# Second unit's low half of each later gate and up half on GpSimd, and five seven-product units in every one of them

## The chip, the cores and the metric

One Trainium2 chip, one of its NeuronCores. The metric is the device time of one execution of the whole program in microseconds (us). Lower is better.

## The reference, cut to what matters

One layer of a residual block on 256 tokens: a half-step feed-forward network, a mixer (a gated recurrence and a short convolution between two projections) and a second half-step feed-forward network. The change touches the gate and up products of the two feed-forward networks only.

```python
D_MODEL = 2048; SEQ = 256; D_FF = 5632; DEPTH = 1
def swiglu(x, w_gate, w_up, w_down):
    return (jax.nn.silu(x @ w_gate) * (x @ w_up)) @ w_down
...
f = swiglu(rmsnorm(h, ffn1_pre_g[l]), ffn1_w_gate[l], ffn1_w_up[l], ffn1_w_down[l])
h = h + 0.5 * rmsnorm(f, ffn1_post_g[l])
...
f = swiglu(rmsnorm(h, ffn2_pre_g[l]), ffn2_w_gate[l], ffn2_w_up[l], ffn2_w_down[l])
h = h + 0.5 * rmsnorm(f, ffn2_post_g[l])
```

## The kernel before, in words

**Number format.** Every float32 operand of a product is split in a high part (a rounded copy, made by ScalarE) and a low part (the difference, made by VectorE). A product is then three matmuls on TensorE: high by high, high by low, low by high (`three`, line 1770). Each of them is a 128x128 block of activations against 512 columns of weights.

**Halves and units.** The first 512 columns of gate and up are made in a plain way. The other 5120 are made in five pairs of 1024 gate columns and 1024 up columns. Each pair has two halves, c = 0 to 9: even c is the gate half, odd c the up half. A half is eight units, p = 0 to 7. A unit is 256 rows of the weights by 1024 columns, taken as a 2x2 matrix of blocks B11, B12, B21, B22 (512 columns each, 1 MB in all), against the 2x2 matrix of the activations (two tiles of rows, two tiles of 128 tokens).

**Seven products or eight.** A plain unit is eight block products, so 24 matmuls. A unit listed in `SEVEN` (line 97) is made with a Strassen-like scheme of seven products, so 21 matmuls. Before the change a half has the seven-product units 2, 4, 6 (c = 0), 0, 2, 3, 4, 6 (c odd) or 0, 2, 4, 6 (c even and above 0). What a seven-product unit asks for beside the matmuls:

- the DMA queue loads B12 early, and then GpSimd issues a second DMA that adds B22's neighbour block into it from DRAM (`pair_sum`, line 689);
- VectorE makes three sums in `tsum` (`half_sums`, line 1235: one instruction of 128x512 and one of 128x1024);
- ScalarE rounds them into `t_hi` (`sums_hi`), VectorE makes `t_lo` (`sums_lo`, line 1250, 128x1536).

`tsum`, `t_hi` and `t_lo` have two places each. So the sums of a unit may be made only when TensorE has finished the seven-product unit two back in the list. That is the wait on `two_back(f, q, p)` (line 437) in `half_sums`.

**Every unit.** ScalarE makes `u_hi` (`half_hi`), VectorE `u_lo` (`half_lo`, line 1228, 128x2048, two inputs in SBUF). The raw weights have four places: the load of unit p waits until TensorE has finished unit p-4.

**VectorE's order in a half** (`half_steps`, line 1286), as written out by hand. First the seven additions of `bank_sums` (line 1255) for the half before, each of which reads one operand from PSUM and one from SBUF. They wait for TensorE at the end of the half before. Then `half_lo` of unit 1, the sums, low half and `t_lo` of unit 2, and so on to unit 7, and last the same for unit 0 of the next half. In gate halves with c above 0 there are two more instructions, `pair_hidden` (line 1193): the elementwise product of gate and up of the pair before. They stand in the order just ahead of `half_lo` of unit 2 and just ahead of `half_lo` of unit 4. TensorE transposes their result after units 3, 4, 5 and 6 of the same half (`pair_transpose`, four small matmuls each).

**GpSimd's order** in this phase is only the row of `pair_sum` DMAs, unit after unit (`pair_sums`, line 696).

**TensorE's order** (`half_unit`, line 1776): unit after unit. Each waits for its low half; the sixth product of a seven-product unit waits for `t_lo`.

The whole is run twice (f = 0 and 1), which makes 160 units and 88 seven-product units.

Of the kernel before, what the change touches and what calls it, by code (L numbers as in the profile page):

```python
# [23 lines left out]
def hybrid_block_kernel(nc, x, f1_pre, f1_wg, f1_wu, f1_wd, f1_post, mix_pre, w_in, conv_w, conv_b,  # L24
                        w_r, b_r, w_i, b_i, lam, sc_w, w_out, mix_post, f2_pre, f2_wg, f2_wu, f2_wd,
                        f2_post, out):
    f32, f32r = mybir.dt.float32, mybir.dt.float32r
    ALU, ACT, AX = mybir.AluOpType, mybir.ActivationFunctionType, mybir.AxisListType
# [13 lines left out]
    GP, GF = KD // GK, KF // GK  # L42
# [51 lines left out]
    HALVES = 2 * PAIRS  # L94
    UNITS = HALVES * GP
    TURN = 4
    SEVEN = [(2, 4, 6)] + [(0, 2, 3, 4, 6) if c % 2 else (0, 2, 4, 6) for c in range(1, HALVES)]
    LAST_SEVEN = SEVEN[0][-1]
    first_seven = [sum(len(x) for x in SEVEN[:c]) for c in range(HALVES + 1)]
    NS = first_seven[HALVES]  # L100
# [20 lines left out]
    EVAC = 7  # L121
# [17 lines left out]
    def lin(q, a, b):  # L139

        it, c = q
        return a * c + b if isinstance(it, int) else it * (TURN * a) + (a * c + b)
# [10 lines left out]
    with ctx:  # L153
# [3 lines left out]
        def sem(name):  # L157
            return ctx.enter_context(nc.semaphore(name))
# [58 lines left out]
        u_raw = [over(f"u_raw{n}", [P, 2, 4, W], f32, a) for n, a in enumerate((resid_at, ring_at))]  # L217
        u_lo = [over(f"u_lo{n}", [P, 2, 4, W], f32r, a) for n, a in enumerate((resid_at, ring_at))]
        u_hi = [over(f"u_hi{n}", [P, 2, 4, W], f32r, a) for n, a in enumerate((ring_at + 2 * ring, ring_at + ring))]
# [34 lines left out]
        def unit(ring_of, p):  # L254
            return ring_of[p % 4 // 2][:, p % 2]
# [89 lines left out]
        pair_raw = {p: sem(f"pair_raw{p}") for p in SEVEN[1]}  # L345
        unit_sum = {p: sem(f"unit_sum{p}") for p in SEVEN[1]}
        pair_used = sem("pair_used")
        unit_hi, unit_lo = sem("unit_hi"), sem("unit_lo")
        unit_used = sem("unit_used")
        sums_done = sem("sums_done")  # L350
        t_hi_done, t_lo_done = sem("t_hi_done"), sem("t_lo_done")
# [2 lines left out]
        evac = sem("evac")  # L354
# [49 lines left out]

        def unit_count(f, q, p):
            return lin(q, GP, UNITS * f + p + 1)

        def turns(q, a, b):

            it, c = q  # L410
            return b if isinstance(it, int) else it * a + b
# [211 lines left out]
        def _(pool):  # L623
# [65 lines left out]
            def pair_sum(f, q, p):  # L689

                first = W + 2 * W * (q // 2)
                pool.wait_ge(pair_raw[p], pair_count(f, (0, q), p))
                pool.dma_start(unit(u_raw, p)[:, B12], ffn_w[f][q % 2][:, GK * p + 1, first:first + W],
                               accum_op=ALU.add).then_inc(unit_sum[p], 16)

            def pair_sums(f):

                for q in range(HALVES):
                    for p in SEVEN[q]:
                        if (q, p) != (0, 2):  # L700
                            pair_sum(f, q, p)

            def down_pairs(f):

# [398 lines left out]
        def _(dve):  # L1103
# [124 lines left out]
            def half_lo(f, q, p):  # L1228
                dve.wait_ge(unit_hi, unit_count(f, q, p))
                if seven(q, p):  # L1230
                    dve.wait_ge(sums_done, sums_count(f, q, p))
                ve.tensor_tensor(unit(u_lo, p), unit(u_raw, p), unit(u_hi, p).bitcast(f32), ALU.subtract  # L1232
                                 ).then_inc(unit_lo, 1)
# [52 lines left out]
            def half_steps(f, q):  # L1286
                it, c = q
                prev, after = (it, c - 1), (it, c + 1)
                if c:
                    bank_sums(f, prev, range(EVAC))  # L1290
                else:
                    hidden(f)
                half_lo(f, q, 1)
                half_sums(f, q, 2)
                if c and c % 2 == 0:
                    pair_hidden(f, prev, 0)
                half_lo(f, q, 2)
                sums_lo(f, q, 2)
                if seven(q, 3):
                    half_sums(f, q, 3)  # L1300
                half_lo(f, q, 3)
                if seven(q, 3):
                    sums_lo(f, q, 3)
                half_sums(f, q, 4)
                if c and c % 2 == 0:
                    pair_hidden(f, prev, 1)
                half_lo(f, q, 4)
                sums_lo(f, q, 4)
                half_lo(f, q, 5)
                if c == 0:  # L1310
                    form_lo_of(f, 7, 8, 9)
                half_sums(f, q, 6)
                half_lo(f, q, 6)
                sums_lo(f, q, 6)
                half_lo(f, q, 7)
                if c < HALVES - 1:
                    seven_first(f, after)
# [336 lines left out]
        def _(pe):  # L1654
# [121 lines left out]
            def half_unit(f, q, p):  # L1776

                c = q[1]
                a12, a22, a11, a21 = ((xT_hi[:, 2 * p + k, part(t)], xT_lo[:, 2 * p + k, part(t)])
                                      for k in range(2) for t in range(2))  # L1780

                def form(name):
                    n = FORM[p, name]
                    return xf[:, n, 0], xf[:, n, 1]

                def raw_of(b):
                    return unit(u_hi, p)[:, b], unit(u_lo, p)[:, b]

                def plain(m, x1, b1, x2, b2):
                    three(bank(m), x1, *raw_of(b1), c == 0 and p == 0, False)  # L1790
                    return three(bank(m), x2, *raw_of(b2), False, p == GP - 1)

                pe.wait_ge(unit_lo, unit_count(f, q, p))
                if c == 0 and p < 3:
                    pe.wait_ge(form_lo, NF * f + (2, 4, 7)[p])
                elif c == 1 and p == 3:
                    pe.wait_ge(form_lo, NF * (f + 1))
                if not seven(q, p):
                    end = p == GP - 1
                    last = plain(M3, form("D1"), B12, form("D2"), B22)  # L1800
                    if end:
                        last.then_inc(bank_done, 1)
                    last = plain(M2, a11, B11, a12, B21)
                    if end:
                        last.then_inc(bank_done, 1)
                    last = plain(M5, a21, B12, a22, B22)
                    if end:
                        last.then_inc(bank_done, 1)
                    last = plain(M4, a21, B11, a22, B21)
                    last.then_inc(unit_used, 1)  # L1810
                    return
                first, end = p == SEVEN[c][0], p == SEVEN[c][-1]
                emptied = first and c > 0
                done = EVAC * (HALVES * f - 1)
                u = seven_sem(q, p)

                def sum_of(b):
                    return t_hi[u][:, b], t_lo[:, u, b]

                def m1():  # L1820
                    if emptied:
                        pe.wait_ge(m1_out, lin(q, 1, HALVES * f))
                    last = three(bank(M1), a11, *raw_of(B11), first, end)
                    if end:
                        last.then_inc(bank_done, 1)

                def m5():
                    if emptied:
                        pe.wait_ge(evac, lin(q, EVAC, done + 6))
                    three(bank(M5), form("S1"), *raw_of(B12), emptied, False).then_inc(pair_used, 1)  # L1830

                if not emptied:
                    m5()
                if not first or c:
                    m1()
                if emptied:
                    pe.wait_ge(evac, lin(q, EVAC, done + 3))
                three(bank(M2), a12, *raw_of(B21), emptied, False)
                if emptied:
                    pe.wait_ge(evac, lin(q, EVAC, done + 4))  # L1840
                three(bank(M3), form("S4"), *raw_of(B22), emptied, False)
                if emptied:
                    m5()
                if first and c == 0:
                    pe.wait_ge(silu_done, TOK * (f + 1))
                    m1()
                pe.wait_ge(t_lo_done, seven_count(f, q, p))
                last = three(bank(M6), form("S2"), *sum_of(U2), first, end)
                if end:
                    last.then_inc(bank_done, 1)  # L1850
                if emptied:
                    pe.wait_ge(evac, lin(q, EVAC, done + 7))
                three(bank(M4), a22, *sum_of(V4), emptied, False)
                if first and c == 0:
                    pe.wait_ge(hid_done, TOK * (f + 1))
                last = three(bank(M7), form("D1"), *sum_of(V3), first, end)
                last.then_inc(unit_used, 1)
# [202 lines left out]
```

## Time and profile before

| what | value |
|---|---|
| median of 3 runs | 1739.95 us (1738.59 to 1741.5) |
| the profiled execution | 1739.42 us |
| its span in the profile | 1737.6 us |
| TensorE matmuls, weight loads | 7728 each |
| share of the span busy: TensorE, VectorE, ScalarE, GpSimd | 99%, 85%, 57%, 10% |
| granted TensorE clock | 0.999 of full speed |

The profiled execution lasts 1.8 us longer than its span; what lies around the span is start and end. A matmul's record is 0.39 us long, but the next one starts 0.23 us after it: the records overlap, so TensorE's time is to be counted by starts, not by durations. VectorE's records overlap too, by about 0.1 us. A "gap" in TensorE is where the distance from one start to the next is more than 0.23 us.

### The profile page before, as it was taken

The page shows a single profiled execution, that of the slowest core. Times are in us where ns is not written, and L with a number is a line of the kernel's source. Part 1 is how long each engine was busy: PE and PEld are TensorE (multiplying, and loading weights), DVE is VectorE, ACT ScalarE, POOL GpSimd, SP SyncE. Part 2 cuts the span into 40 slices and gives each one's busy share as a digit, 9 for nine tenths or more (in the row PEclk, how much of TensorE's full clock was granted, in tenths as well). Part 3 has the DMA queues.
Part 4 walks back from the last instruction along what each step waited for, and adds up shares of the span by engine and source line. Part 5 has one row for each costly group of instructions (what it writes and reads, how often), then busy time and mean ns, then how long its engine had stood idle before and what let it go on. Part 6 is the DMA issues. An engine that isn't in the chain of part 4 may idle for free.

```text
span 1737.6 us, 21090 instructions
## 1 busy us (share of the span) xinstructions
PE 1721.0 (99%) x7728; PEld 1419.3 (82%) x7728; DVE 1470.5 (85%) x1297; ACT 993.3 (57%) x951; POOL 170.0 (10%) x160
## 2 busy tenths in 40 slices
PE   9999999999999999999999999999999999999997
PEld 7778888888888888788888888888888888888886
DVE  6999999999899877755685558999999999988786
ACT  7665656555656444756654447565656565655543
POOL 5300000000000000100000018001010111000000
PEclk9999999999999999999999999999999999999999
DMA  7788778787767667575565557787878787677665
GB/s 240 224 235 229 226 229 241 221 242 220 219 206 232 215 201 252 177 232 174 164 195 180 192 183 248 212 239 226 238 223 242 229 236 227 197 222 234 204 199 201
DMA packets 148517, 378.15 MB, mean 218 GB/s; under 512 B 12364, under 2 KB 14548, under 8 KB 147668
## 3 DMA queue, kind: packets, MB, share of 16 engines
q1 hardware_dynamic: 133716, 350.33, 61.6%
q0 software_dynamic: 14688, 26.75, 9.9%
q8 instruction: 49, 0.80, 0.2%
q14 instruction: 32, 0.26, 0.1%
q10 hardware_dynamic: 32, 0.01, 0.0%
HBM read 372.84 MB, written 4.19 MB: 217 GB/s over the span
## 4 chain that ended last, share of the span: by engine, by line
PE 93%; DVE 2%; DMA 2%; issue 1%; ACT 0%; POOL 0%; SPq 0%; DVEq 0%; ACTq 0%
PE ps L1772 23%; PE ps L1774 23%; PE ps L1773 23%; PE ps L1662 7%; PE ps L1664 7%; PE ps L1663 7%; PE ps L1767 1%; DMA u_raw<-in_ffn_w_gate 1%; DVE w_lo L1117 1%; DVE u_lo L1232 1%; DMA u_raw<-in_ffn_w_up 1%; PE ps L1981 1%; DMA raw<-in_ffn_w_gate 0%; PE ps L1993 0%; PE ps L1703 0%
## 5 line engine op out<-in xcount | busy, mean ns | idle before, releaser
L842 ACT CAST u_hi<-u_raw 128x2048 fp32r<-128x2048 f32 x160 | 305.8, 1913 | 167.0 <-DMA u_raw<-in_ffn_w_gate 80.7
L1232 DVE TENSOR_TENSOR u_lo<-u_raw,u_hi 128x2048 fp32r<-128x2048 f32 x160 | 367.4, 2296 | 11.6 <-ACT u_hi L842 4.5
L1117 DVE TENSOR_TENSOR w_lo<-raw,w_hi 128x1024 fp32r<-128x1024 f32 x156 | 195.9, 1262 | 134.4 <-ACT w_hi L743 132.3
L743 ACT CAST w_hi<-raw 128x1024 fp32r<-128x1024 f32 x160 | 166.7, 1052 | 138.1 <-PE ps L1664 111.5
L1772 PE MATMUL ps<-u_hi,xT_hi 128*128 128x512 f32 x608 | 237.0, 390 | 0.0
L1774 PE MATMUL ps<-u_hi,xT_lo 128*128 128x512 f32 x608 | 236.9, 390 | 0.0
L1773 PE MATMUL ps<-u_lo,xT_hi 128*128 128x512 f32 x608 | 236.7, 389 | 0.0
L1006 ACT CAST d_hi<-d_raw 128x2048 fp32r<-128x2048 f32 x80 | 152.8, 1913 | 115.9 <-DVE d_raw L1450 60.8
L1443 DVE TENSOR_TENSOR d_lo<-d_raw,d_hi 128x2048 fp32r<-128x2048 f32 x80 | 182.9, 2288 | 15.1 <-ACT d_hi L1006 12.0
L849 ACT CAST t_hi<-tsum 128x1536 fp32r<-128x1536 f32 x88 | 130.7, 1485 | 107.0 <-DVE tsum L1247 106.2
L1662 PE MATMUL ps<-w_hi,xT_hi 128*128 128x512 f32 x448 | 178.3, 398 | 2.6 <-DVE xT_lo L1153 2.3
L1772 PE MATMUL ps<-d_hi,hT_all 128*128 128x512 f32 x460 | 179.2, 390 | 0.0
L1774 PE MATMUL ps<-d_hi,hT_all 128*128 128x512 f32 x460 | 179.1, 389 | 0.0
L1773 PE MATMUL ps<-d_lo,hT_all 128*128 128x512 f32 x460 | 179.0, 389 | 0.0
L1664 PE MATMUL ps<-w_hi,xT_lo 128*128 128x512 f32 x448 | 174.9, 390 | 0.0
L1663 PE MATMUL ps<-w_lo,xT_hi 128*128 128x512 f32 x448 | 174.5, 390 | 0.0
L1253 DVE TENSOR_TENSOR t_lo<-tsum,t_hi 128x1536 fp32r<-128x1536 f32 x88 | 154.2, 1752 | 20.2 <-ACT t_hi L849 20.2
L1773 PEld LDWEIGHTS ps<-u_lo,xT_hi 128*128 128x128 f32 x608 | 114.2, 188 | 24.2
L1774 PEld LDWEIGHTS ps<-u_hi,xT_lo 128*128 128x128 f32 x608 | 114.2, 188 | 24.0
L1772 PEld LDWEIGHTS ps<-u_hi,xT_hi 128*128 128x128 f32 x608 | 114.2, 188 | 24.0
L1772 PE MATMUL ps<-u_hi,xf 128*128 128x512 f32 x320 | 129.1, 404 | 2.3 <-DVE u_lo L1232 1.2
L1774 PE MATMUL ps<-u_hi,xf 128*128 128x512 f32 x320 | 125.0, 391 | 0.0
(207 smaller groups left out, 3049.8 us busy)
## 6 DMA issues: line engine op xcount, KB each, us to landing
d_raw<-in_ffn_w_down SPq DMA_DIRECT2D x50, 1024.0 KB, 5.3
u_raw<-in_ffn_w_gate SPq DMA_DIRECT2D x42, 1024.0 KB, 5.2
raw<-in_w_in SPq DMA_DIRECT2D x80, 512.0 KB, 3.7
u_raw<-in_ffn_w_up SPq DMA_DIRECT2D x30, 1024.0 KB, 5.2
u_raw<-in_ffn_w_up SPq DMA_DIRECT2D x100, 256.0 KB, 4.2
u_raw<-in_ffn_w_up SPq DMA_DIRECT2D x50, 512.0 KB, 3.7
u_raw<-in_ffn_w_gate SPq DMA_DIRECT2D x76, 256.0 KB, 4.1
u_raw<-in_ffn_w_gate SPq DMA_DIRECT2D x38, 512.0 KB, 3.7
```

Of the source, the lines that this page charges most:

```text
L743: sc.copy(w_hi[:, s], raw[:, s]).then_inc(hi_ready, 1)
L842: sc.copy(unit(u_hi, p), unit(u_raw, p)).then_inc(unit_hi, 1)
L1117: ve.tensor_tensor(w_lo[:, s], raw[:, s], w_hi[:, s].bitcast(f32), ALU.subtract).then_inc(lo_ready, 1)
L1232: ve.tensor_tensor(unit(u_lo, p), unit(u_raw, p), unit(u_hi, p).bitcast(f32), ALU.subtract).then_inc(unit_lo, 1)
L1253: ve.tensor_tensor(t_lo[:, u], tsum[:, u], t_hi[u][:].bitcast(f32), ALU.subtract).then_inc(t_lo_done, 1)
L1443: ve.tensor_tensor(d_lo[n][:], d_raw[n][:], d_hi[n][:].bitcast(f32), ALU.subtract).then_inc(d_lo_done, 1)
L1662: te.matmul(dst, xh, w_hi[:, s, k], start=start and k == 0, stop=False)
L1663: te.matmul(dst, xh, w_lo[:, s, k], start=False, stop=False)
L1664: last = te.matmul(dst, xl, w_hi[:, s, k], start=False, stop=stop and k == GK - 1)
L1772: te.matmul(dst, xs[0], hi, start=start, stop=False)
L1773: te.matmul(dst, xs[0], lo, start=False, stop=False)
L1774: return te.matmul(dst, xs[1], hi, start=False, stop=stop)
```

## The change

GpSimd gets a function `second_lo`: for every half but the first it makes the low half of unit 1, in two instructions of 128x1024. It may start when `u_hi` of unit 1 is there and when the first of the seven bank sums of the half before is done. It stands in GpSimd's order behind the `pair_sum` of unit 2 and ahead of that of the next seven-product unit. VectorE no longer makes this low half, and TensorE waits for `pool_lo` in its place. `SEVEN` gets unit 3 in the gate halves c = 2, 4, 6 and 8 too.

```diff
-    SEVEN = [(2, 4, 6)] + [(0, 2, 3, 4, 6) if c % 2 else (0, 2, 4, 6) for c in range(1, HALVES)]
+    SEVEN = [(2, 4, 6)] + [(0, 2, 3, 4, 6)] * (HALVES - 1)
...
-        unit_hi, unit_lo = sem("unit_hi"), sem("unit_lo")
+        unit_hi, unit_lo, pool_lo = sem("unit_hi"), sem("unit_lo"), sem("pool_lo")
...
+        def lo_by_pool(c, p):
+            return c > 0 and p == 1
+
+        def lo_done(f, q, p):
+            own = [[not lo_by_pool(c, r) for r in range(GP)] for c in range(HALVES)]
+            half = sum(own[1])
+            if lo_by_pool(q[1], p):
+                return pool_lo, turns(q, TURN, (HALVES - 1) * f + q[1])
+            n = sum(sum(x) for x in own) * f + sum(sum(x) for x in own[:q[1]]) + sum(own[q[1]][:p + 1])
+            return unit_lo, turns(q, TURN * half, n)
...
                     for p in SEVEN[q]:
                         if (q, p) != (0, 2):
                             pair_sum(f, q, p)
+                        if q and p == 2:
+                            second_lo(f, q)
+
+            def second_lo(f, q):
+
+                b, lo, hi = unit(u_raw, 1), unit(u_lo, 1), unit(u_hi, 1)
+                pool.wait_ge(unit_hi, unit_count(f, (0, q), 1))
+                pool.wait_ge(evac, EVAC * (HALVES * f + q - 1) + 1)
+                pool.tensor_tensor(lo[:, 0:2], b[:, 0:2], hi[:, 0:2].bitcast(f32), ALU.subtract)
+                pool.tensor_tensor(lo[:, 2:4], b[:, 2:4], hi[:, 2:4].bitcast(f32), ALU.subtract).then_inc(pool_lo, 1)
...
-                half_lo(f, q, 1)
+                if not lo_by_pool(c, 1):
+                    half_lo(f, q, 1)
                 half_sums(f, q, 2)
...
-                pe.wait_ge(unit_lo, unit_count(f, q, p))
+                pe.wait_ge(*lo_done(f, q, p))
```

How the order moves in the gate half c = 2. VectorE before, from the last bank sum to the low half of unit 4 (`u_raw0` and `u_raw1` are the two pairs of places of the raw weights, units 0, 1 (and 4, 5) and units 2, 3 (and 6, 7)):

```order
L1283 TENSOR_TENSOR hid_x<-ps,hid_x 128x512
L1232 TENSOR_TENSOR u_lo0_59<-u_raw0_57,u_hi0_61 128x2048
L1245 TENSOR_TENSOR tsum_54<-u_raw1_58 128x512
L1247 TENSOR_TENSOR tsum_54<-u_raw1_58,tsum_54 128x1024
L1197 SCALAR_TENSOR_TENSOR hid<-hid,rstd,act_g 128x1024
L1232 TENSOR_TENSOR u_lo1_60<-u_raw1_58,u_hi1_62 128x2048
L1253 TENSOR_TENSOR t_lo_55<-tsum_54,t_hi1_64 128x1536
L1232 TENSOR_TENSOR u_lo1_60<-u_raw1_58,u_hi1_62 128x2048
L1245 TENSOR_TENSOR tsum_54<-u_raw0_57 128x512
L1247 TENSOR_TENSOR tsum_54<-u_raw0_57,tsum_54 128x1024
L1197 SCALAR_TENSOR_TENSOR hid_x<-hid_x,rstd,act_x_56 128x1024
L1232 TENSOR_TENSOR u_lo0_59<-u_raw0_57,u_hi0_61 128x2048
```

The same stretch of VectorE now:

```order
L1304 TENSOR_TENSOR hid_x<-ps,hid_x 128x512
L1266 TENSOR_TENSOR tsum_54<-u_raw1_58 128x512
L1268 TENSOR_TENSOR tsum_54<-u_raw1_58,tsum_54 128x1024
L1218 SCALAR_TENSOR_TENSOR hid<-hid,rstd,act_g 128x1024
L1253 TENSOR_TENSOR u_lo1_60<-u_raw1_58,u_hi1_62 128x2048
L1274 TENSOR_TENSOR t_lo_55<-tsum_54,t_hi1_64 128x1536
L1266 TENSOR_TENSOR tsum_54<-u_raw1_58 128x512
L1268 TENSOR_TENSOR tsum_54<-u_raw1_58,tsum_54 128x1024
L1253 TENSOR_TENSOR u_lo1_60<-u_raw1_58,u_hi1_62 128x2048
L1274 TENSOR_TENSOR t_lo_55<-tsum_54,t_hi0_63 128x1536
L1266 TENSOR_TENSOR tsum_54<-u_raw0_57 128x512
L1268 TENSOR_TENSOR tsum_54<-u_raw0_57,tsum_54 128x1024
```

The low half of unit 1 is gone from behind the bank sums. The sums and the `t_lo` of unit 3, three instructions, have come in between the low half of unit 2 and the sums of unit 4; the second `pair_hidden` and the low half of unit 4 follow behind the last row shown, as before.

GpSimd in the same half, before: the DMAs of units 0, 2, 4 and 6.

```order
L693 DMA u_raw0_57<-in_ffn1_w_gate 128x512
L693 DMA u_raw1_58<-in_ffn1_w_gate 128x512
L693 DMA u_raw0_57<-in_ffn1_w_gate 128x512
L693 DMA u_raw1_58<-in_ffn1_w_gate 128x512
```

And now, units 0, 2, (unit 1's low half), 3, 4, 6:

```order
L704 DMA u_raw0_57<-in_ffn1_w_gate 128x512
L704 DMA u_raw1_58<-in_ffn1_w_gate 128x512
L721 TENSOR_TENSOR u_lo0_59<-u_raw0_57,u_hi0_61 128x1024
L722 TENSOR_TENSOR u_lo0_59<-u_raw0_57,u_hi0_61 128x1024
L704 DMA u_raw1_58<-in_ffn1_w_gate 128x512
L704 DMA u_raw0_57<-in_ffn1_w_gate 128x512
L704 DMA u_raw1_58<-in_ffn1_w_gate 128x512
```

The two subtractions stand between the DMA of unit 2 and the new DMA of unit 3.

## Rows read from the trace of the kernel before

**Rows 1.** The page's part 1: busy us, share of the span, instructions.

```profile
PE 1721.0 (99%) x7728; PEld 1419.3 (82%) x7728; DVE 1470.5 (85%) x1297; ACT 993.3 (57%) x951; POOL 170.0 (10%) x160
```

**Rows 2.** Who waited for whom, TensorE: total us, times, longest.

```profile
PE ps L1772 <- DVE u_lo L1232: 1.2, 2, 0.9
```

**Rows 3.** Timeline, TensorE, gate half c = 2: start us, duration us, engine, line, tiles.

```profile
142.57 0.39 PE L1772 MATMUL ps<-u_hi,xT_hi 128*128 128x512 f32 x1
...
157.53 0.39 PE L1772 MATMUL ps<-u_hi,xf 128*128 128x512 f32 x1
...
162.75 0.39 PE L1774 MATMUL ps<-u_hi,xT_lo 128*128 128x512 f32 x1
...
163.33 0.48 PE L1772 MATMUL ps<-u_hi,xf 128*128 128x512 f32 x1
...
185.31 0.39 PE L1772 MATMUL ps<-u_hi,xT_hi 128*128 128x512 f32 x1
```

**Rows 4.** Timeline, VectorE, gate half c = 2.

```profile
139.82 0.68 DVE L1263 TENSOR_TENSOR hid<-ps,hid 128x512 f32<-128x512 f32 x1
...
144.14 2.28 DVE L1232 TENSOR_TENSOR u_lo<-u_raw,u_hi 128x2048 fp32r<-128x2048 f32 x1
146.34 0.68 DVE L1245 TENSOR_TENSOR tsum<-u_raw 128x512 f32<-128x512 f32 x1
...
149.39 2.29 DVE L1232 TENSOR_TENSOR u_lo<-u_raw,u_hi 128x2048 fp32r<-128x2048 f32 x1
...
153.26 2.29 DVE L1232 TENSOR_TENSOR u_lo<-u_raw,u_hi 128x2048 fp32r<-128x2048 f32 x1
155.46 0.69 DVE L1245 TENSOR_TENSOR tsum<-u_raw 128x512 f32<-128x512 f32 x1
...
158.52 2.28 DVE L1232 TENSOR_TENSOR u_lo<-u_raw,u_hi 128x2048 fp32r<-128x2048 f32 x1
```

**Rows 5.** Timeline, VectorE and TensorE, up half c = 3, units 3 and 4.

```profile
194.31 0.68 DVE L1245 TENSOR_TENSOR tsum<-u_raw 128x512 f32<-128x512 f32 x1
...
196.35 2.30 DVE L1232 TENSOR_TENSOR u_lo<-u_raw,u_hi 128x2048 fp32r<-128x2048 f32 x1
...
200.57 0.69 DVE L1245 TENSOR_TENSOR tsum<-u_raw 128x512 f32<-128x512 f32 x1 [0.25 <-PE ps L1774]
...
202.62 2.29 DVE L1232 TENSOR_TENSOR u_lo<-u_raw,u_hi 128x2048 fp32r<-128x2048 f32 x1
...
200.04 0.39 PE L1774 MATMUL ps<-t_hi,xf 128*128 128x512 f32 x1
...
205.03 0.44 PE L1772 MATMUL ps<-u_hi,xf 128*128 128x512 f32 x1
```

**Rows 6.** GpSimd's groups by line, 695 to 1100 us: busy us, mean ns.

```profile
L644 POOL TENSOR_TENSOR w_lo<-raw,w_hi 128x1024 fp32r<-128x1024 f32 x4 | 9.5, 2386 | 15.2 <-ACT w_hi L743 15.2
```

**Rows 7.** Timeline, GpSimd beside VectorE, 1078 to 1083 us.

```profile
1078.51 1.59 POOL L678 TENSOR_TENSOR xf<-x,xf 128x512 f32<-128x512 f32 x1
...
1078.99 3.38 DVE L1232 TENSOR_TENSOR u_lo<-u_raw,u_hi 128x2048 fp32r<-128x2048 f32 x1 [1.46 <-ACT u_hi L842]
```

**Rows 8.** Timeline, what unit 1's low half will follow: c = 2, then c = 6.

```profile
139.50 1.91 ACT L842 CAST u_hi<-u_raw 128x2048 fp32r<-128x2048 f32 x1 [2.12 <-DMA u_raw<-in_ffn_w_gate]
140.25 0.86 POOL L693 DMA_DIRECT2D u_raw<-in_ffn_w_gate  x1 [9.94 <-DMA u_raw<-in_ffn_w_gate]
...
303.82 1.92 ACT L842 CAST u_hi<-u_raw 128x2048 fp32r<-128x2048 f32 x1 [0.57 <-DMA u_raw<-in_ffn_w_gate]
...
308.46 0.39 PE L1772 MATMUL ps<-u_hi,xT_hi 128*128 128x512 f32 x1
```

**Rows 9.** Timeline, GpSimd, the DMA of unit 3 in the up half c = 3.

```profile
188.72 0.86 POOL L693 DMA_DIRECT2D u_raw<-in_ffn_w_up  x1 [7.46 <-DMA u_raw<-in_ffn_w_up]
```

**Rows 10.** Timeline, up half c = 1: TensorE's first matmul, VectorE's sums of unit 3.

```profile
100.84 0.39 PE L1772 MATMUL ps<-u_hi,xT_hi 128*128 128x512 f32 x1
...
111.71 0.69 DVE L1245 TENSOR_TENSOR tsum<-u_raw 128x512 f32<-128x512 f32 x1 [1.08 <-issue]
```

## The prediction

> **What bounds the kernel now.** I began with the busy times. TensorE is busy 99% of the span, VectorE 85%, GpSimd 10% [rows 1]. The list of waits says that TensorE waited 1.2 us in all for `u_lo` [rows 2]. So TensorE's matmuls set the time, and a matmul less is time won, but only where its inputs stay ahead. The shares don't tell how far ahead they are, so I read the starts in one gate half. I count from T, TensorE's first matmul of the half: 142.57 us for c = 2. Units 0, 1 and 2 are 21 + 24 + 21 = 66 matmuls, and unit 3 starts at T+14.96 (157.53): 0.2267 us a matmul [rows 3]. Unit 3, still plain, has its last start at T+20.18, and unit 4 begins at T+20.76, behind four small transposes [rows 3].
>
> VectorE runs close ahead of that. In the up half c = 3 the low half of unit 4 ends at 204.91 and TensorE takes it at 205.03, 0.12 us later [rows 5]. What holds it there is a chain: VectorE may make the sums of unit 4 only when TensorE is through with unit 2, because unit 3 has the other place. They start 0.53 us after the last start of unit 2 (200.04, 200.57), with a wait shown [rows 5]. In the gate half c = 2, where unit 3 is plain, nothing of this exists, and the low half of unit 4 ends at 160.80, 2.5 us ahead of its use [rows 3, 4]. This spare is what the change spends.
>
> **Fewer matmuls.** Four gate halves in each of two networks get one more seven-product unit: 8 units, 3 matmuls each, 24 x 0.2267 = **-5.4 us**. Nothing else on TensorE is changed, so this is certain as long as it isn't made to wait.
>
> **VectorE in a gate half.** It loses the low half of unit 1: from 144.14 to the next start at 146.34, 2.20 us [rows 4]. It gains sums and `t_lo` of unit 3: sums to low half 2.04 us (194.31 to 196.35) [rows 5] and `t_lo` 1.67 us, which is the 3.87 us from one low half over `t_lo` to the next instruction (149.39 to 153.26) less those 2.20 [rows 4]. So it has 3.71 us more and 2.20 less ahead of the sums of unit 4. Let S be the start of the sums of unit 2, from T. Then the low half of unit 2 starts at S+3.05 (146.34 to 149.39, `pair_hidden` included), the sums of unit 3 at +3.87, its low half at +2.04, the sums of unit 4 at +3.87, its low half at +3.06 (155.46 to 158.52, the second `pair_hidden` included) [rows 4, 5]. That is S+15.89; it ends 2.29 later, and TensorE can go 0.12 after that: S+18.30. TensorE would be ready at T+20.76 - 0.68 = T+20.08. **It waits S - 1.78 us at unit 4, in every one of the eight gate halves.** The same two-places wait sets a floor now: sums of unit 4 not before T+14.74+0.53 = T+15.27, hence unit 4 not before 15.27+3.06+2.29+0.12 = T+20.74, a wait of 0.66 us however early VectorE is. The floor rules for S under 2.44.
>
> **When GpSimd lets VectorE go.** Bank sums end as now, and VectorE would start the sums of unit 2 at T+1.57 (144.14). But GpSimd is then reading SBUF. No row shows `second_lo`; the nearest is GpSimd's own `w_lo` of 128x1024, the same subtraction on the same types, 2.39 us mean of four [rows 6]. Two make 4.77 us. The far bound is its 128x512 of 1.59 us [rows 7], four of them, 6.4 us; that one is another operand form and small, so I stay with the four of the same form. Below 4.7 nothing speaks.
>
> The Trainium skill, GPSIMD Engine Reference, section 3.1, gives 4497 ns for a `tensor_tensor` of 2048 float32 elements; by that figure, an estimate, S would be 0.27 earlier and the total some 2 us lower.
>
> Does VectorE wait for it? The trace has one clean meeting. GpSimd starts a 128x512 at 1078.51 for 1.59 us, so to 1080.10; VectorE's `u_lo` starts at 1078.99 and lasts 3.38 us where it otherwise takes 2.29 [rows 4, 7]. It is 1.09 us longer, and GpSimd's instruction had 1.11 us to go. So an instruction of VectorE with two inputs in SBUF stands still until GpSimd's is through. I take that at full price. The bank sums have one input in PSUM; I cost them at nothing.
>
> The Trainium skill, SBUF — State Buffer, section "Who interferes with whom", states both: two SBUF inputs block against GpSimd's reads, at most one does not. Its rule that the first to issue keeps the port through its whole instruction would let VectorE's first sum in between the two subtractions, if it were asked for ahead of the second; that would be a saving of at most one subtraction, and is weighed below as a rival by its row.
>
> GpSimd starts when three things are done. The first bank sum: T-2.75 + 0.68 = T-2.07 [rows 4]. Its DMA of unit 2: 140.25 + 0.86, T-1.46 in c = 2 [rows 8]. And `u_hi` of unit 1: 141.41 or T-1.16 in c = 2, but 305.74 or T-2.72 in c = 6 [rows 3, 8]. Over the eight gate halves this `u_hi` ends like the first once (T-1.2), like the second five times (T-2.65 to T-2.8), and twice between, at T-1.5. With 0.1 us for a semaphore, GpSimd starts at T-1.05, T-1.4 (twice) and T-1.95 (five times), and S is 3.7, 3.4 and 2.8. So VectorE's gain from the missing low half is nearly eaten: sums of unit 2 stand at T+3.77 now (146.34) [rows 4]. The waits are 1.9 + 2 x 1.6 + 5 x 1.05 = **+10.4 us**.
>
> Unit 1 itself is no danger: its low half is ready at S, and TensorE takes it at T+4.76 (21 matmuls).
>
> **Up halves.** There too VectorE gets ahead by the missing low half, but the sums of unit 4 wait for TensorE's unit 2 as they do now [rows 5]. Nothing won, nothing lost. It follows that the gate half after it begins with VectorE where it is today.
>
> **The new DMA.** B12 of unit 3 is loaded when TensorE leaves unit 7 of the half before. In the up half the DMA that adds to it goes out at T+3.41 (188.72, T = 185.31), and the sums follow at T+9.0 without a wait [rows 3, 5, 9]. In the gate half GpSimd has the subtractions ahead of it, done at S at the latest, about the same time; the sums of unit 3 are wanted at S+6.92 = T+9.7 to 10.6. Cost nothing, cover 0.7 to 1.6 us. If the cover is gone each us late is a us of waiting. ScalarE has one more `t_hi` of 1.5 us and is 57% busy [rows 1]: nothing.
>
> **Sum.** -5.4 + 10.4 = +5.0 us on the profiled execution's 1739.42, so 1744.4. The median of the runs shown is 0.5 above that execution: **1744.9 us**. Own range of this case: all eight waits at 1.05 give 1742.9, all at 1.9 give 1749.7, and the far bound for the subtractions would add 1.6 each, 13 us; as the row of the same form is so much nearer, I reach only a little above: 1742.5 to 1751. About 0.2% (3.5 us) is what a measurement of this kernel can tell from no change.
>
> **Rivals.**
>
> 1. *GpSimd doesn't hold VectorE here* (it is through early, or VectorE's sum slips in ahead of the second subtraction). For it: in c = 2 the second subtraction would start at T+1.3, close to VectorE's T+1.57. Against it: in five of eight it starts at T+0.4, and the meeting above. S is then under 2.44 and the floor stands: 8 x 0.66 = 5.3 against 5.4, so 1739.8. This is the other side of my forecast: not slower.
> 2. *TensorE never waits.* Clean gain, 1734.5. It needs the two-places wait to cost nothing with `pair_hidden` behind it; the up half shows that chain with no us to spare even without `pair_hidden` [rows 5]. Only something I misread in the order brings this.
> 3. *The DMA of unit 3 is late.* In the up half c = 1 the sums of unit 3 came at T+10.87 after 1.08 us idle [rows 10]. If that were the rule in the gate halves, the wait would be 10.87 - 9.74 = 1.1 us more than 1.05 in each: 8 x 2.2 - 5.4 = +12.2, 1752. Against it: it shows in one up half of ten.
>
> **How the numbers follow.** Forecast 0.60, rival 1 0.20, rival 2 0.08, rival 3 0.12. Slower by over 0.2% (above 1743.4): rival 3 and four fifths of the forecast, 0.60. Within: rival 1 and the rest, 0.32. Faster: 0.08. The range reaches down over rival 1, to 1738.8, and up to 1751, where it takes in half of the way to rival 3.
>
> **What the changed profile would show.** Right: 7704 matmuls; at unit 4 of each gate half a gap of 1 to 2 us more than the transposes', ended by VectorE's `u_lo`; the first sum of unit 2 in gate halves longer than 0.69 us, up to about 2, and ending with GpSimd's second subtraction; that sum of unit 2 in up halves held only until about T+1.5; sums of unit 4 in up halves still waiting for TensorE. Wrong: no gap at unit 4; gaps at unit 1 (GpSimd late) or unit 3 (DMA late); subtractions much longer or shorter than 2.39 us; bank sums lengthened beside GpSimd.

## The result, and the profile after

| | before | changed |
|---|---|---|
| median of 22 runs each | 1739.66 us | 1742.72 us |
| lowest to highest | 1736.9 to 1741.67 | 1739.75 to 1747.94 |
| profiled execution | 1739.42 us | 1744.52 us |
| matmuls | 7728 | 7704 |

The ratio is 1.0019, 95% interval 1.0013 to 1.0024: the change is slower by 3.1 us, with 24 matmuls less. The profiled execution is slower by 5.1 us. Where the difference between median and profile may come from is told below.

The changed kernel's page, part 1, beside [rows 1]:

```profile
PE 1718.0 (99%) x7704; PEld 1415.3 (81%) x7704; DVE 1475.1 (85%) x1303; ACT 1005.5 (58%) x959; POOL 263.2 (15%) x204
```

Only GpSimd's busy time has moved much. The list of TensorE's waits beside [rows 2] says more: engine, who it waited for, total us, times, longest.

```profile
PE ps L1794 <- DVE u_lo L1253: 10.1, 13, 1.4
```

Where, the timeline of the gate half c = 6 of the first network shows. T is 309.65. GpSimd, then VectorE, then TensorE:

```profile
307.75 2.40 POOL L721 TENSOR_TENSOR u_lo<-u_raw,u_hi 128x1024 fp32r<-128x1024 f32 x1 [0.96 <-DVE hid L1284]
310.12 2.40 POOL L722 TENSOR_TENSOR u_lo<-u_raw,u_hi 128x1024 fp32r<-128x1024 f32 x1
```

```profile
310.63 0.68 DVE L1304 TENSOR_TENSOR hid_x<-ps,hid_x 128x512 f32<-128x512 f32 x1
311.23 1.85 DVE L1266 TENSOR_TENSOR tsum<-u_raw 128x512 f32<-128x512 f32 x1
313.11 1.23 DVE L1268 TENSOR_TENSOR tsum<-u_raw,tsum 128x1024 f32<-128x1024 f32 x1
...
325.25 0.68 DVE L1266 TENSOR_TENSOR tsum<-u_raw 128x512 f32<-128x512 f32 x1
...
328.30 2.28 DVE L1253 TENSOR_TENSOR u_lo<-u_raw,u_hi 128x2048 fp32r<-128x2048 f32 x1
```

```profile
309.65 0.39 PE L1794 MATMUL ps<-u_hi,xT_hi 128*128 128x512 f32 x1
...
329.14 0.39 PE L1796 MATMUL ps<-t_hi,xf 128*128 128x512 f32 x1
329.37 0.60 PE L1789 MATMUL ps<-ident,hid 128*128 128x128 f32 x4
330.64 0.50 PE L1794 MATMUL ps<-u_hi,xf 128*128 128x512 f32 x1 [0.68 <-DVE u_lo L1253]
```

The bank sum at 310.63 is 0.68 us long, as before, with GpSimd's subtraction running beside it. The first sum of unit 2 is 1.85 us long instead of 0.69: it is held for 1.16 us, until GpSimd's second subtraction is about through (312.52; the sum, taken as its usual 0.69 us before its end, would start at 312.39). The sums of unit 4 start at T+15.60 and the low half ends at 330.58. Unit 3's last matmul starts at 329.14, unit 4's first at 330.64, 1.50 us later, where the transposes alone account for 0.58 [rows 3]. So TensorE waits **0.92 us**.

Counted in this way over the whole trace (last start of a unit, first start of the next, less what stood there before), the eight gate halves lose 1.68, 1.03, 0.92, 0.92 us in the first network and 2.81, 1.52, 0.92, 0.90 in the second, together 10.7 us. The up halves c = 1 lose 1.13 us in the two networks together, where they lost 1.34 before. The matmuls give 5.44. The sum, 10.7 - 5.44 - 0.2 = +5.1, is the difference of the two profiled executions; other halves differ by up to 0.6 us either way, and these nearly cancel.

The four dear gate halves all have a late transfer in the trace, each in another place. In c = 2 of the first network it makes `u_hi` of unit 1 late (T-1.12 instead of about T-2.7). In c = 4 of the first network the DMA of unit 2 goes out a microsecond late. In c = 4 of the second a late load in the up half before delays ScalarE, then VectorE's bank sums by 0.6 us. In c = 2 of the second network (T = 1167.86) the DMA of unit 2 goes out late, GpSimd's subtractions end at T+3.4, and the accumulating DMA of unit 3 needs over 7 us; VectorE stands idle for its sums:

```profile
1165.61 0.88 POOL L704 DMA_DIRECT2D u_raw<-in_ffn_w_gate  x1 [11.21 <-DMA u_raw<-in_ffn_w_gate]
1166.18 2.74 POOL L721 TENSOR_TENSOR u_lo<-u_raw,u_hi 128x1024 fp32r<-128x1024 f32 x1
1168.54 2.73 POOL L722 TENSOR_TENSOR u_lo<-u_raw,u_hi 128x1024 fp32r<-128x1024 f32 x1
1172.18 0.89 POOL L704 DMA_DIRECT2D u_raw<-in_ffn_w_gate  x1 [0.91 <-DMA u_raw<-in_ffn_w_gate]
```

```profile
1179.55 0.69 DVE L1266 TENSOR_TENSOR tsum<-u_raw 128x512 f32<-128x512 f32 x1 [1.40 <-issue]
```

The two subtractions are also slower here, 2.7 us instead of 2.4. In all traces with 128x1024 subtractions, one lasts 2.39 to 2.43 us, except where GpSimd's DMA just ahead of it is hardly over. With 0.11 us of that DMA's record still to run at its start the first of the two lasts 2.54 (c = 4 of the first network), with 0.20 us 2.63 (run 4 below), with 0.30 us 2.74 (here). In these three the second is as long as the first. Why, no run shows.

Late transfers fall on other halves in the traces of the other versions. If none were late, eight waits of 0.92 less the matmuls would make +1.9; the profiled execution, with four dearer ones, has +5.1; the median of +3.1 lies between. That the median run has fewer late transfers than the profiled one is likely, but not shown: the other executions have no trace.

In the up halves the gain on VectorE goes nowhere, as forecast. In c = 7 the sums of unit 4 wait 1.41 us for TensorE to be through with unit 2, where the wait was 0.25 before, as in [rows 5]:

```profile
367.89 0.69 DVE L1266 TENSOR_TENSOR tsum<-u_raw 128x512 f32<-128x512 f32 x1 [1.41 <-PE ps L1796]
```

### The profile page after: what moved, and what is told of

It reads as the page before. It is cut to its first block, busy times and chain, and to the rows that moved or that the text cites. A ratio compares the mean times of both kernels' runs of the same rounds, so it can differ in the third digit from the quotient of the medians.

```text
span 1742.7 us, 21144 instructions
## 1 busy us (share of the span) xinstructions
PE 1718.0 (99%) x7704; PEld 1415.3 (81%) x7704; DVE 1475.1 (85%) x1303; ACT 1005.5 (58%) x959; POOL 263.2 (15%) x204
## 4 chain that ended last, share of the span: by engine, by line
PE 77%; DVE 10%; DMA 7%; issue 4%; POOL 1%; ACT 1%; DVEq 0%; SPq 0%; ACTq 0%
PE ps L1794 18%; PE ps L1796 18%; PE ps L1795 18%; PE ps L1684 7%; PE ps L1686 7%; PE ps L1685 7%; DMA u_raw<-in_ffn_w_gate 6%; DVE u_lo L1253 4%; DVE t_lo L1274 1%; DVE tsum L1266 1%; DVE tsum L1268 1%; DVE w_lo L1138 1%; DMA u_raw<-in_ffn_w_up 1%; PE ps L1789 1%; DMA d_raw<-in_ffn_w_down 1%
## 5 line engine op out<-in xcount | busy, mean ns | idle before, releaser
L1253 DVE TENSOR_TENSOR u_lo<-u_raw,u_hi 128x2048 fp32r<-128x2048 f32 x142 | 327.9, 2309 | 11.1 <-ACT u_hi L863 3.1
L1794 PE MATMUL ps<-u_hi,xT_hi 128*128 128x512 f32 x576 | 224.4, 390 | 0.0
L1796 PE MATMUL ps<-u_hi,xT_lo 128*128 128x512 f32 x576 | 224.3, 389 | 0.0
L1795 PE MATMUL ps<-u_lo,xT_hi 128*128 128x512 f32 x576 | 224.1, 389 | 0.0
L870 ACT CAST t_hi<-tsum 128x1536 fp32r<-128x1536 f32 x96 | 142.6, 1486 | 96.8 <-DVE tsum L1268 95.4
L1274 DVE TENSOR_TENSOR t_lo<-tsum,t_hi 128x1536 fp32r<-128x1536 f32 x96 | 168.1, 1751 | 5.1 <-ACT t_hi L870 5.1
L1794 PEld LDWEIGHTS ps<-u_hi,xT_hi 128*128 128x128 f32 x576 | 108.2, 188 | 22.8
L1795 PEld LDWEIGHTS ps<-u_lo,xT_hi 128*128 128x128 f32 x576 | 108.1, 188 | 22.8
L1796 PEld LDWEIGHTS ps<-u_hi,xT_lo 128*128 128x128 f32 x576 | 108.1, 188 | 22.8
```

What stands on the lines that cost most here:

```text
L1274: ve.tensor_tensor(t_lo[:, u], tsum[:, u], t_hi[u][:].bitcast(f32), ALU.subtract).then_inc(t_lo_done, 1)
L1794: te.matmul(dst, xs[0], hi, start=start, stop=False)
L1795: te.matmul(dst, xs[0], lo, start=False, stop=False)
L1796: return te.matmul(dst, xs[1], hi, start=False, stop=stop)
```

## The experiments

Each version was timed against the kernel before on the same chip. Its medians are 1739.68 (runs 1 to 4), 1739.97 (5 to 8) and 1739.81 (9 and 10). The theory is the prediction's: the new sums of unit 3 and the two-places wait make VectorE late at unit 4, and GpSimd's reading takes back a large part of what the off-load gives. The rivals are that the off-load itself costs, and that something else (ScalarE, a transfer, the order alone) rules.

**1. Off-load alone**, with the old list.

```diff
-    SEVEN = [(2, 4, 6)] + [(0, 2, 3, 4, 6)] * (HALVES - 1)
+    SEVEN = [(2, 4, 6)] + [(0, 2, 3, 4, 6) if c % 2 else (0, 2, 4, 6) for c in range(1, HALVES)]
```

> The low half of unit 1 on GpSimd, but the old list of seven-product units. My theory (the two-places chain at unit 4 of the gate halves eats the saved matmuls, and GpSimd frees VectorE early by next to nothing): no wait at unit 4 in the gate halves, since unit 3 is plain there and the low half of unit 4 had 2.5 us to spare; the kernel before is matched within 2 us, 1737.5 to 1740. Rival (GpSimd's subtractions themselves hurt, by holding VectorE or by coming late): waits at units 1, 2 or 4 and a time above 1742.

1739.13 us, ratio 0.9998 (0.9989 to 1.0007). In its c = 6, unit 3's last start (328.08) and unit 4's first (328.66) are 0.58 us apart: no wait, and none in the other seven. The off-load alone neither costs nor gives anything that can be measured, though GpSimd holds VectorE there too (the first sum of unit 2 is 1.86 us long in c = 6).

**2. The new list alone**: the kernel before with the reverse of that diff.

> The new list of seven-product units, but all low halves on VectorE. The sums of unit 2 then stand at T+3.77 and the wait at unit 4 is 3.77 - 1.78 = 2.0 us in each gate half: 8 x 2.0 - 5.4 = +10.5 us, about 1750 (1748 to 1752). Rival (the off-load is what costs, the sevens pay): about 1734.5, faster than before.

1748.83 us, ratio 1.0055 (1.0042 to 1.0069). In c = 6 (T = 310.10) the sums of unit 2 start at T+3.77, and 2.27 us lie between unit 3's last start and unit 4's first, 0.58 of them the transposes':

```profile
313.87 0.68 DVE L1245 TENSOR_TENSOR tsum<-u_raw 128x512 f32<-128x512 f32 x1
...
329.85 0.39 PE L1774 MATMUL ps<-t_hi,xf 128*128 128x512 f32 x1
...
332.12 0.50 PE L1772 MATMUL ps<-u_hi,xf 128*128 128x512 f32 x1 [1.44 <-DVE u_lo L1232]
```

Every gate half waits 1.6 to 1.7 us at unit 4 and 0.1 or more at unit 3, 14.8 us in the eight. The expectation had 2.0 at unit 4 and didn't count that unit 3 takes a part of it. The rival is out: the sevens are what costs, and the off-load softens it.

**3. GpSimd without reading.**

```diff
-                pool.tensor_tensor(lo[:, 0:2], b[:, 0:2], hi[:, 0:2].bitcast(f32), ALU.subtract)
-                pool.tensor_tensor(lo[:, 2:4], b[:, 2:4], hi[:, 2:4].bitcast(f32), ALU.subtract).then_inc(pool_lo, 1)
+                pool.memset(lo.bitcast(f32), 0.0).then_inc(pool_lo, 1)
```

> The changed kernel with the two subtractions replaced by one fill with zeros, which reads nothing from SBUF; the low half of unit 1 is left out of the result. If it is GpSimd's reading that holds VectorE, the sums of unit 2 start at T+1.57 without being lengthened, the floor of the two-places wait rules and the wait at unit 4 is 0.66 us in all eight gate halves: 5.3 against 5.4, about 1739.5 (1738.5 to 1741). If GpSimd doesn't hold VectorE, nothing changes against the changed kernel, 1742 to 1744. If the two-places wait is no floor, 1734 to 1736.

1737.16 us, ratio 0.9992 (0.9983 to 1.0001). VectorE's and TensorE's timeline in c = 6 (T = 307.38):

```profile
308.94 0.68 DVE L1265 TENSOR_TENSOR tsum<-u_raw 128x512 f32<-128x512 f32 x1
...
322.63 0.69 DVE L1265 TENSOR_TENSOR tsum<-u_raw 128x512 f32<-128x512 f32 x1 [0.76 <-PE ps L1795]
...
326.87 0.39 PE L1795 MATMUL ps<-t_hi,xf 128*128 128x512 f32 x1
...
328.04 0.50 PE L1793 MATMUL ps<-u_hi,xf 128*128 128x512 f32 x1 [0.34 <-DVE u_lo L1252]
```

The first sum starts at T+1.56 and is 0.68 long. VectorE then waits 0.76 us for TensorE, at T+15.25, and TensorE still waits 1.17 - 0.58 = 0.59 us at unit 4. All eight gate halves show 0.58 or 0.59. That is the floor of the two-places wait, seen by itself. By these waits the run should be 0.8 us faster than the kernel before; the median is 2.5 us faster and lies below the expected range, but the ratio's interval (-3.0 to +0.2 us) holds the 0.8. The fill is also shorter (1.81 us) and is over before VectorE comes, so this run doesn't say that a longer fill would leave VectorE alone: that it is GpSimd's reading that holds VectorE, and not its being busy, isn't shown.

**4. The second elementwise product later.**

```diff
-                if c and c % 2 == 0:
-                    pair_hidden(f, prev, 1)
                 half_lo(f, q, 4)
                 sums_lo(f, q, 4)
+                if c and c % 2 == 0:
+                    pair_hidden(f, prev, 1)
```

> The changed kernel with the second elementwise product of gate and up moved from ahead of the low half of unit 4 to behind the t_lo of unit 4. It takes 1.19 us out of the chain that ends at unit 4. With the sums of unit 2 at T+2.9 the low half of unit 4 ends near T+20.1 and the wait shrinks from 0.92 to about 0.1 us; with the sums at T+3.7 from 1.7 to 0.7. Sum of the eight waits about 2 to 3 us instead of 10.7: about 1735 (1733.5 to 1737), faster than both kernels. Rival (TensorE is held at unit 4 by something else, ScalarE or a DMA): no change, 1742 to 1744. If the elementwise product is then late for the transposes, a new gap in front of unit 6 or 7.

1736.18 us, ratio 0.9983 (0.9974 to 0.9992). In c = 6 nothing is left but the transposes, 0.59 us from 327.74 to 328.33:

```profile
325.90 2.29 DVE L1253 TENSOR_TENSOR u_lo<-u_raw,u_hi 128x2048 fp32r<-128x2048 f32 x1
...
327.74 0.39 PE L1796 MATMUL ps<-t_hi,xf 128*128 128x512 f32 x1
327.97 0.60 PE L1789 MATMUL ps<-ident,hid 128*128 128x128 f32 x4
328.33 0.48 PE L1794 MATMUL ps<-u_hi,xf 128*128 128x512 f32 x1
```

Three of the eight gate halves keep waits of 0.3 to 0.65 us, two with a late `u_hi` of unit 1. The third is c = 2 of the first network (0.47 us), where the subtractions take 2.63 us, and where the low half of unit 4 starts 0.46 us after the sums, against 0.1 elsewhere; what holds it there stays open. VectorE's chain was what ended the common wait; ScalarE and the DMAs matter only where they make that chain late.

**5. GpSimd earlier.**

```diff
-                pool.wait_ge(evac, EVAC * (HALVES * f + q - 1) + 1)
```

> The changed kernel, but GpSimd's two subtractions no longer wait for the first bank sum, only for the high part of unit 1 (and for their place behind the DMA of unit 2). In the five or six gate halves where the high part is there at T-2.7, GpSimd would start at T-2.6 instead of T-1.9, the sums of unit 2 follow at T+2.2 instead of T+2.9, and the wait at unit 4 falls from 0.92 us to the floor that the run with a fill in place of the subtractions showed, 0.59. Six times 0.33 is 2 us: about 1741 (1739.5 to 1742.5). Where the high part comes late nothing changes. Rival (meeting VectorE's t_lo of unit 0 costs more than it brings): 1743 or more, with lengthened t_lo records.

1741.71 us, ratio 1.0012 (1.0004 to 1.0021). In four of the eight gate halves the wait is 0.58, the floor; the others keep 0.7 to 1.4. The four are those where `u_hi` of unit 1, the DMA of unit 2 or VectorE itself is late. In c = 6 (T = 309.29) the subtractions start at T-2.62 instead of T-1.90, VectorE's sum is held for 0.44 us only, and the sums of unit 4 again wait for TensorE:

```profile
309.03 2.41 POOL L721 TENSOR_TENSOR u_lo<-u_raw,u_hi 128x1024 fp32r<-128x1024 f32 x1
...
310.86 1.13 DVE L1265 TENSOR_TENSOR tsum<-u_raw 128x512 f32<-128x512 f32 x1
```

GpSimd ends 0.73 us earlier than in the changed kernel (T+2.15, T+2.88) and the sum's effective start moves by the same (T+2.01, T+2.74). TensorE's wait gets only 0.34 us of it, then the floor stops it. The time is as expected, but its interval overlaps the changed kernel's: the gain is read from the trace.

**6. One subtraction for two.**

```diff
-                pool.tensor_tensor(lo[:, 0:2], b[:, 0:2], hi[:, 0:2].bitcast(f32), ALU.subtract)
-                pool.tensor_tensor(lo[:, 2:4], b[:, 2:4], hi[:, 2:4].bitcast(f32), ALU.subtract).then_inc(pool_lo, 1)
+                pool.tensor_tensor(lo, b, hi.bitcast(f32), ALU.subtract).then_inc(pool_lo, 1)
```

> The changed kernel with one subtraction of 128x2048 in place of two of 128x1024. The Trainium skill, GPSIMD Engine Reference, section 3.1, gives 4497 ns for 2048 elements, against the two that take 4.77 us in the changed kernel's own trace. If the page's figure holds here, the sums of unit 2 come 0.25 us earlier and the eight waits shrink by that: 2 us in all, about 1741. If the two records already overlap, nothing changes, 1742 to 1743.5.

1741.92 us, ratio 1.0012 (1.0003 to 1.0021). Group by line:

```profile
L721 POOL TENSOR_TENSOR u_lo<-u_raw,u_hi 128x2048 fp32r<-128x2048 f32 x18 | 83.6, 4645 | 13.0 <-DVE act_g L1283 7.8 <-DVE hid L1283 4.7 <-ACT u_hi L862 0.5
```

4.65 us, against 4.77 from the start of the first to the end of the second. The 4.50 of the Trainium skill (GPSIMD Engine Reference, section 3.1), which is for an addition, isn't reached. In c = 6 (T = 311.03) the first sum is shorter by 0.14, and the wait at unit 4 is 0.76 instead of 0.92:

```profile
312.60 1.71 DVE L1265 TENSOR_TENSOR tsum<-u_raw 128x512 f32<-128x512 f32 x1
```

The step is seen in the trace, but this run's time can't be told from the changed kernel's.

**7. The new list and the later product, no off-load**: the second kernel of this list with the edit of the fourth.

> No off-load, the new list, and the second elementwise product behind the t_lo of unit 4. From the run with the new list alone (waits of 0.1 at unit 3 and 1.68 at unit 4 of each gate half): the product takes 1.19 out of the chain at unit 4, so 0.5 to 0.6 us is left there and 0.1 at unit 3: 8 x 0.65 = 5.2 against 5.4 saved: 1739.5 (1738.5 to 1741). Rival (the off-load brings nothing): the same as with the off-load and the later product, 1736.

1742.98 us, ratio 1.0018 (1.0007 to 1.0028). A miss: the expectation was 1739.5. The waits at units 3 and 4 of the gate halves are 0.8 us each, 6.3 in all, where 5.2 were expected. What was left out is small and frequent. After a wait at unit 3, one matmul starts 0.34 us after the one before instead of 0.23. And the up halves behind a gate half now lose about 0.1 us each: the product, moved back, makes their bank sums end 0.4 us later (T+1.39 instead of T+0.96 in c = 7), and there VectorE has nothing to spare. The two profiled executions differ by 2.2 us (1741.66 and 1739.42); why the median is 0.8 us further off isn't shown. Beside run 4 (ratios 1.0018 and 0.9983) it prices the off-load: some 6 us, once the product is out of the way.

**8. A shared low half and the later product.** GpSimd makes the first 128x1024 of unit 1's low half, VectorE the second behind the bank sums; TensorE waits for both. The edit of run 4 is in it too, and VectorE's call for the low half of unit 1 stands in every half again.

```diff
-            return c > 0 and p == 1
+            return False
...
-                pool.tensor_tensor(lo[:, 0:2], b[:, 0:2], hi[:, 0:2].bitcast(f32), ALU.subtract)
-                pool.tensor_tensor(lo[:, 2:4], b[:, 2:4], hi[:, 2:4].bitcast(f32), ALU.subtract).then_inc(pool_lo, 1)
+                pool.tensor_tensor(lo[:, 0:2], b[:, 0:2], hi[:, 0:2].bitcast(f32), ALU.subtract).then_inc(pool_lo, 1)
...
-                ve.tensor_tensor(unit(u_lo, p), unit(u_raw, p), unit(u_hi, p).bitcast(f32), ALU.subtract
+                n = 2 if q[1] and p == 1 else 0
+                ve.tensor_tensor(unit(u_lo, p)[:, n:], unit(u_raw, p)[:, n:], unit(u_hi, p)[:, n:].bitcast(f32), ALU.subtract
...
                 pe.wait_ge(*lo_done(f, q, p))
+                if c and p == 1:
+                    pe.wait_ge(pool_lo, turns(q, TURN, (HALVES - 1) * f + c))
```

> The best version so far (off-load, new list, second product later), but GpSimd makes only the first half of unit 1's low part and VectorE the second behind the bank sums. VectorE is then through at T+1.57+1.15 = T+2.7 whenever GpSimd starts before T-0.8, where two subtractions give T+2.9 to T+4.2. The two or three gate halves with a late high part should lose their waits (0.5, 0.3 and 0.65 us beyond the transposes in the run before), the others none: 1735 (1733.5 to 1736.5). Rival (VectorE's extra 1.15 us in each half costs elsewhere): 1736.5 or more.

1733.44 us (1732.12 to 1734.93, five runs), ratio 0.9963 (0.995 to 0.9976), the fastest version and just under the expected range. Timeline of c = 6 (T = 306.47), GpSimd and VectorE:

```profile
304.56 2.40 POOL L721 TENSOR_TENSOR u_lo<-u_raw,u_hi 128x1024 fp32r<-128x1024 f32 x1 [0.89 <-DVE hid L1284]
...
308.04 1.21 DVE L1253 TENSOR_TENSOR u_lo<-u_raw,u_hi 128x1024 fp32r<-128x1024 f32 x1
309.17 0.68 DVE L1266 TENSOR_TENSOR tsum<-u_raw 128x512 f32<-128x512 f32 x1
```

GpSimd is through at T+0.5, a microsecond before VectorE starts its own part. Nothing is held, and the sums of unit 2 stand at T+2.70, in c = 2 of the second network too, where `u_hi` ends late, at T-1.38. Six gate halves have no wait. Two have 0.1 and 0.3; in these VectorE's own bank sums end 0.3 and 0.4 us late.

**9. The later product in the kernel before**: the edit of run 4 alone.

> The kernel before with nothing but the second elementwise product behind the t_lo of unit 4. There the low half of unit 4 had 2.5 us to spare in the gate halves, so taking 1.19 us out of its chain should bring nothing: 1738.5 to 1741, no difference. Rival (the order of the product is a gain of its own, and the list of units has nothing to do with it): 1736 or less.

1738.77 us, ratio 0.9995 (0.9986 to 1.0004). No gain of its own that can be measured: the product's place matters with the new list.

**10. The shared low half, product in its old place**: run 8 without the edit of run 4.

> The changed kernel with unit 1's low half shared (first half GpSimd, second half VectorE), the second elementwise product ahead of the low half of unit 4 as before. The sums of unit 2 start at T+2.7 to T+2.8 in all gate halves, the wait at unit 4 is then 0.8 to 1.0 us in each, with no dearer ones where the high part of unit 1 comes late: 8 x 0.9 - 5.4 = +1.8 us, about 1741.5 (1740.5 to 1743). Against the changed kernel a gain of about 1 us; against the shared low half with the later product 7 to 8 us more, which is then the price of the product's place. Rival (sharing is what made that version fast): 1736 or less.

1740.11 us, ratio 1.0004 (0.9995 to 1.0013). Eight waits of 0.83 to 0.93 us, none dearer. That is a little below the expected range. By the ratios (1.0004 and 0.9963) the product's place is worth about 7 us. Beside the changed kernel (1.0019), sharing is worth 2.6 us, though in a half with nothing late its wait (0.85 in c = 6) is nearly the same as there (0.92): what it takes away are the dear halves. This trace has fewer late transfers than the changed kernel's, so how much is due to sharing is not settled by it alone; run 8 beside run 4 (0.9963, 0.9983) has 3.5 us the same way.

## Why the prediction was right

**The time.** Forecast 1744.9 (+5.0), measured 1742.72 (+3.1). That is close to the lower end of what the prediction's own terms span (1742.5), and inside the band of 0.2% that it called "within" and gave 0.32; it had given "slower" 0.60. The interval of the ratio still has the changed kernel slower.

**Direction and mechanism.** Slower, because the matmuls saved are given back at unit 4 of the gate halves. Runs 1 and 2 show that the new list brings the wait, run 4 that VectorE's chain is what ends it, run 3 that the two-places wait is its floor.

**Fewer matmuls.** 7704, as said; 5.44 us.

**VectorE's chain.** From the effective start of the sums of unit 2 (313.11 - 0.72 = T+2.74) to the sums of unit 4 (T+15.60) it is 12.86, forecast 12.83; on to TensorE 5.39, forecast 5.47.

**GpSimd's hold.** Forecast S = T+2.8 in the common case, measured T+2.74. The wait was forecast at 1.05 and is 0.92. The subtractions take 2.43 us in the mean, not 2.39. "Nearly eaten" is too strong for the common case: from T+3.77 to T+2.74 VectorE keeps 1.03 of the 2.20 us. In up halves the hold ends at T+1.35 (353.51 + 1.16 - 0.69 in c = 7), forecast T+1.5. Bank sums keep their 0.68 us, as assumed.

**The floor.** 0.66 forecast, 0.58 measured.

**Which halves are dear.** This is the term that was off. The prediction took from one trace three of eight gate halves as late for good and came to 10.4 us of waits. The profiled execution has 10.7, but that agreement is luck, for it is made up otherwise: of the five halves forecast at 1.05 four cost 0.92, the fifth (c = 4 of the second network) is late too and costs 1.52, and a wait at unit 3 comes from a late DMA, which was rival 3. The median is 2 us less slow than that execution. The forecast of +5.0 against +3.1 measured is most likely this mis-sized term: the common case is +1.9, and the rest is drawn anew in each run.

**The new DMA**, at no cost: right in seven of eight gate halves of the trace; 1.13 us at unit 3 in the eighth, one of the prediction's own signs of being wrong.

**Rivals.** The first (not held, 1739.8) is out by the 1.16 us in c = 6. Its second form, VectorE's sum slipping in ahead of the second subtraction, was never put to the test: in every gate half of the changed kernel that subtraction had begun at least 0.7 us before VectorE came. The second rival (1734.5) needed the product moved, which the change doesn't do; run 8, with it moved and no wait left in six gate halves, is 6.4 us faster than the kernel before by its ratio, which agrees with the 5.4 of the matmuls within its interval. The third showed in one gate half.

**Left open.** No version with a third place for `tsum`, `t_hi` and `t_lo` was run, so the price of the two places is known only as the 0.58 us that run 3 leaves at unit 4.

## What to carry to other kernels

Work given to a second engine is paid for where it meets the first one. Here GpSimd making half of the subtraction, done before VectorE started the other half, was worth some 3 us more than GpSimd making the whole of it, and, as the traces have it, not in the ordinary halves but in those where something came late: a part that is through a microsecond early can be late without anyone waiting. When units are converted to save TensorE's time, list what each one adds to the helper's order ahead of the next deadline, and look for a wait on a ring of two places that becomes adjacent; then move whatever isn't due yet behind that deadline. An average share (VectorE 85%, the same before and after) shows none of this.

## What the runs showed of the hardware that I had not expected

GpSimd's subtraction of 128x2048 takes 4.65 us in one instruction, 4.77 in two, so an instruction more costs only 0.12 us. A held instruction of VectorE shows up as a long record (1.85 for 0.69 us), not as idle time, so a list of waits or of busy shares counts it as work. GpSimd's subtraction keeps its 2.40 us beside bank sums that read one input from PSUM, and these keep their 0.68. It was longer (2.54 to 2.74) where it started before the record of GpSimd's own DMA ahead of it was over.
